# Four buffers for expert results, and the gather of the fifth expert ahead issued before each scatter

## The reference

```
h      = rmsnorm(x1, g_ffn)                                   # 512 x 1024
scores = sigmoid(h @ w_router)                                # 64 experts
top_idx = top_k(scores + router_bias, 8);  gates = normalised scores * 2.5
y  = sum over experts e of  gates[:, e] * (silu(h @ w_gate_e[e]) * (h @ w_up_e[e])) @ w_down_e[e]
y += (silu(h @ w_gate_s) * (h @ w_up_s)) @ w_down_s           # shared expert
out = x1 + y
```

## Time and profile before

| | us |
|---|---|
| median of 3 runs (1119.38 to 1122.89) | 1120.4 |
| the profiled execution | 1125.33 |
| its span, first to last instruction | 1123.3 |
| TensorE busy with matmuls | 1089.0 (97%) |
| VectorE busy | 881.5 (78%) |
| ScalarE busy | 738.1 (66%) |
| GpSimd busy | 326.3 (29%) |

### The profile page before, as it was taken

The page is one execution under the profiler, slowest core; times in us unless marked ns, Lnnn a source line. Parts: engine busy times, 40 slices in busy tenths (PEclk is TensorE's granted clock), DMA queues, the critical chain, the costliest instruction groups (busy, mean ns, idle before and its releaser), DMA issues.

```text
span 1123.3 us, 19070 instructions
## 1 busy us (share of the span) xinstructions
PE 1089.0 (97%) x5809; PEld 894.5 (80%) x5809; DVE 881.5 (78%) x1405; ACT 738.1 (66%) x1304; POOL 326.3 (29%) x293
## 2 busy tenths in 40 slices
PE   7999999999999999999999999999999999999995
PEld 6789978777777887478888788888888788888884
DVE  6544385578766835589999999999998999999993
ACT  5434465444446422268888888888888888888883
POOL 1221021000000001126336633333344545534543
PEclk9999999999999999999999999999999999999998
DMA  7243211421522185459999999999999999999962
GB/s 245 77 110 111 81 52 63 150 76 48 159 77 95 62 341 209 171 229 400 374 383 377 376 376 392 381 371 369 375 374 376 380 365 369 375 382 376 376 202 36
DMA packets 69704, 284.69 MB, mean 253 GB/s; under 512 B 16611, under 2 KB 19179, under 8 KB 44700
## 3 DMA queue, kind: packets, MB, share of 16 engines
q1 hardware_dynamic: 51228, 250.50, 57.3%
q0 software_dynamic: 18432, 33.61, 12.8%
HBM read 279.79 MB, written 37.81 MB: 283 GB/s over the span
## 4 chain that ended last, share of the span: by engine, by line
DMA 49%; PE 32%; DVE 7%; issue 5%; POOL 3%; ACT 2%; POOLq 1%; SPq 0%; ACTq 0%; DVEq 0%
DMA out<-arena,idxs 48%; PE bank L1647 21%; PE bank L1795 3%; POOL turn L592 2%; PE bank L1591 2%; PE bank L1809 2%; DVE w_lo L1082 1%; ACT arena L782 1%; DMA arena<-in_w_in 1%; DVE gu_parts L1433 1%; PE bank L1703 1%; PE bank L1716 1%; PE bank L1905 1%; ACT w_hi L681 1%; PE bank L1692 1%
## 5 line engine op out<-in xcount | busy, mean ns | idle before, releaser
L1821 PE MATMUL bank<-gu_parts,xT_parts 128*128 128x512 f32 x1280 | 339.0, 395 | 3.3 <-DVE xT_parts L1426 1.6
L1821 PEld LDWEIGHTS bank<-gu_parts,xT_parts 128*128 128x128 f32 x1280 | 235.3, 188 | 51.0 <-DVE xT_parts L1426 2.7
L1835 PE MATMUL bank<-w_lo 128*128 128x512 f32 x804 | 201.5, 399 | 1.0 <-DVE w_lo L1439 1.0
L592 POOL TENSOR_TENSOR turn<-minus_half 16x1 f32<-16x1 f32 x128 | 101.6, 794 | 345.8 <-DMA out<-arena,idxs 292.7
L1835 PEld LDWEIGHTS bank<-w_lo 128*128 128x128 f32 x804 | 146.3, 188 | 29.7 <-DVE w_lo L1439 1.1
L1647 PE MATMUL bank<-w_hi,hT_hi 128*128 128x512 f32 (+1 forms) x320 | 125.0, 391 | 2.3 <-DVE w_lo L1082 2.3
L1647 PE MATMUL bank<-w_hi,hT_lo 128*128 128x512 f32 (+1 forms) x320 | 122.5, 383 | 0.0
L1647 PE MATMUL bank<-w_lo,hT_hi 128*128 128x512 f32 (+1 forms) x320 | 122.1, 382 | 0.0
L602 POOL DMA_INDIRECT out<-arena,idxs x64 | 110.4, 1725 | 26.7 <-issue 23.8
L1433 DVE TENSOR_TENSOR gu_parts<-arena_x,gu_parts 128x1024 fp32r<-128x1024 f32 x96 | 117.0, 1218 | 1.3 <-ACT gu_parts L953 1.2
L1433 DVE TENSOR_TENSOR gu_parts<-arena,gu_parts 128x1024 fp32r<-128x1024 f32 x96 | 117.0, 1219 | 0.0
(11 more groups left out here) (226 smaller groups left out, 1958.4 us busy)
## 6 DMA issues: line engine op xcount, KB each, us to landing
arena<-in_w_gate_e SPq DMA_DIRECT2D x32, 1024.0 KB, 8.9
arena<-in_w_up_e SPq DMA_DIRECT2D x32, 1024.0 KB, 12.3
arena<-in_w_down_e SPq DMA_DIRECT2D x32, 1024.0 KB, 7.4
arena_x<-in_w_gate_e SPq DMA_DIRECT2D x32, 1024.0 KB, 9.0
arena_x<-in_w_up_e SPq DMA_DIRECT2D x32, 1024.0 KB, 12.2
arena_x<-in_w_down_e SPq DMA_DIRECT2D x32, 1024.0 KB, 7.1
arena<-in_w_in SPq DMA_DIRECT2D x14, 1024.0 KB, 5.4
arena<-in_w_gate SPq DMA_DIRECT2D x8, 1024.0 KB, 5.8
```

Source lines behind the costliest of these rows:

```text
L592: nc.gpsimd.tensor_tensor(turn[:], minus_half[0:16, 0:1], minus_half[0:16, 0:1], ALU.add).then_inc(turns, 1)
L1821: last = nc.tensor.matmul(out_, a[:, PER * c + j, :], b[c][:, :, j, :], start=(c == 0 and j == 0 and i == 0), stop=(c == CHUNKS - 1 and j ...
L1835: last = nc.tensor.matmul(psY[h][0:rows, :], midT[n][a][:, j, 0:rows], w[b][:, j, h * 512:(h + 1) * 512], start=(j == 0 and k == 0), stop= ...
```

## The change

Results get two more buffers: one at 20 KB of the arena, and a new tile `y_more` in the space that the tile `w_lo` has and the expert stage doesn't need. `pos` gets a tile of its own, since 23 KB is now under a result buffer. ScalarE's `y_i` takes the slot in place of the parity and waits for experts 0 to k-4 in place of 0 to k-2; the wait of `keep_idx` stays as it is. In GpSimd's `pair` the gather of expert k+5 stands before the scatter of expert k, with the numbers of their turns exchanged.

```diff
--- before.py
+++ after.py
@@ -177,6 +177,7 @@
         idxs = [sb(f"idxs{i}", [P, 1], u32) for i in range(4)]
         hn_ss, hn_ms, hn_r = sb("hn_ss", [P, NT]), sb("hn_ms", [P, NT]), sb("hn_r", [P, NT])
         rbias = sb("rbias", [P, E])
+        pos = sb("pos", [P, NT, E])[:]
 
         KB = 256
         with ExitStack() as view_ctx:
@@ -186,7 +187,9 @@
         arena = sb("arena", [P, 121 * KB])
 
 
-        w_lo = sb("w_lo", [P, RING, N], mybir.dt.float32r)
+        with ExitStack() as lo_ctx:
+            w_lo = lo_ctx.enter_context(nc.sbuf_tensor("w_lo", [P, RING, N], mybir.dt.float32r))
+        down_parts, y_more = sb("down_parts", [P, 20 * KB], mybir.dt.float32r), sb("y_more", [P, 4 * KB])
         with ExitStack() as split_ctx:
             hT_hi, hT_lo, w_hi = (split_ctx.enter_context(nc.sbuf_tensor(name, [P, blocks, N], mybir.dt.float32r))
                                   for name, blocks in (("hT_hi", ND), ("hT_lo", ND), ("w_hi", RING)))
@@ -250,11 +253,10 @@
 
         wgu = [at(k, 2 * ND * F).rearrange("p (g j c) -> p g j c", g=2, j=ND) for k in (40, 121, 153, 0)]
         wd = [at(k, NF * D).rearrange("p (j c) -> p j c", j=NF) for k in (56, 137, 169, 64)]
-        y = [at(24 + 4 * i, D) for i in range(2)]
+        y = [at(24, D), at(28, D), at(20, D), y_more[:]]
         xg = [at(72 + 4 * i, D) for i in range(4)]
         table = at(145, NT * E * 3).bitcast(bf16).rearrange("p (t e c) -> p t e c", t=NT, e=E)
 
-        down_parts = w_lo[:].rearrange("p b c -> p (b c)")
         wd_hi, wd_lo = (down_parts[:, i * NF * D:(i + 1) * NF * D].rearrange("p (j c) -> p j c", j=NF) for i in range(2))
         last_hi, last_lo = (gu_parts[:, k * KB:k * KB + NF * D].rearrange("p (j c) -> p j c", j=NF) for k in (8, 16))
         midT = [[down_parts[:, 2 * NF * D + (2 * i + k) * NF * P:2 * NF * D + (2 * i + k + 1) * NF * P].rearrange("p (j s) -> p j s", j=NF)
@@ -271,7 +273,6 @@
         sel, rep, M, gt, gres = (at(16 + i, NT * E).rearrange("p (t e) -> p t e", t=NT) for i in range(5))
         scores = at(24, NT * E).rearrange("p (t e) -> p t e", t=NT)
         Mb = at(22, NT * E // 2).bitcast(bf16).rearrange("p (t e) -> p t e", t=NT)
-        pos = at(23, NT * E).rearrange("p (t e) -> p t e", t=NT)
         wr = at(112, ND * E).rearrange("p (j e) -> p j e", j=ND)
 
         bank = [ctx.enter_context(nc.psum_tensor(f"bank{i}", [P, 512], f32)) for i in range(8)]
@@ -612,7 +613,7 @@
                 pool.wait_ge(y_ready, 2 * (SH + k + 1))
                 pool.wait_ge(idx_kept, k + 1)
                 after(pool, scattered, 16 * k)
-                scatter(u % 2, idxs[u], before, scattered)
+                scatter(u, idxs[u], before, scattered)
 
             for k in range(5):
                 gather_k(k, k % 4, k)
@@ -620,8 +621,8 @@
                 pool.wait_ge(b, 8 * SH)
 
             def pair(k, u):
-                scatter_k(k, u, 5 + 2 * k)
-                gather_k(k + 5, (u + 1) % 4, 6 + 2 * k)
+                gather_k(k + 5, (u + 1) % 4, 5 + 2 * k)
+                scatter_k(k, u, 6 + 2 * k)
 
             for k in range(4):
                 pair(k, k)
@@ -925,11 +926,11 @@
                 after(act, mid_ready, it - 1)
                 silu_of(n).then_inc(silu_ready, 1)
 
-            def y_i(it, n):
-                after(act, scattered, 16 * (it - SH - 1))
+            def y_i(it, slot):
+                after(act, scattered, 16 * (it - SH - 3))
                 for h in range(2):
                     act.wait_ge(y_psum, 2 * it + h + 1)
-                    copy_y(n, h).then_inc(y_ready, 1)
+                    copy_y(slot, h).then_inc(y_ready, 1)
 
             def midT_i(it, n, rows):
                 act.wait_ge(midT_psum, it + 1)
@@ -979,12 +980,12 @@
                     for h in range(2):
                         split_wd(slot, h, last_hi).then_inc(wd_hi_ready, 1)
                     midT_i(it, n, SLOTS)
-                    y_i(it - 1, 1 - n)
+                    y_i(it - 1, (slot + 3) % 4)
                     return
                 if more:
                     xT_hi_k(k + 1)
                     gu_hi_k(k + 1, (slot + 1) % 4, CHUNKS - 1)
-                y_i(it - 1, 1 - n)
+                y_i(it - 1, (slot + 3) % 4)
                 midT_i(it, n, SLOTS)
                 wd_i(it, slot)
 
@@ -1023,7 +1024,7 @@
                     step(4 * m + u, u % 2, u)
             for it in range(ITEMS - 4, ITEMS):
                 step(it, it % 2, it % 4, more=it + 1 < ITEMS)
-            y_i(ITEMS - 1, 1)
+            y_i(ITEMS - 1, 3)
 
             more = act.value_load(rounds_i[0:1, 0:1], min_val=0, max_val=ROUNDS - 1)
             with act.If(more > 0):
```

## The result

The changed kernel takes 1187.5 us (median of 6 runs, 1166.98 to 1192.61), the kernel before, on the same chip, 1120.9 (6 runs, 1116.65 to 1125.38): **slower, by a ratio of 1.0466 [1.0421, 1.0511]**. The prediction was 1109 us, range 1105 to 1121, with 0.65 for faster. The sign, the size and the range are wrong. The profiled execution took 1187.38, a span of 1185.4, which is 62.1 us over the span of before.

A forecast was written before the change was run, and what follows sets the result against it. It took TensorE's 9.53 us a step, plus scatter-chain delays through ScalarE, as the bound. Minus 13.1 and +1.0 for slips gave -12.1 on 1125.3, 1113.2; runs' median 4.9 lower, 1108.3, taken as 1109 us, range 1105 to 1121.

The forecast's parts named there:

- The reading of the bound: Expert stage: TensorE's 9.53 us a step bounds it, plus what the scatter chain adds through ScalarE; 13.1 us lost.
- The two limits: ScalarE's waits for scatters: the result copy's goes, `keep_idx` is next in line, so room gained is 3.65 us.
- After, it settles by itself: Scatter chain: late scatters are followed sooner, so offsets settle near 4.5 to 5, below the new limit of 7.2; minus 13.1 us.
- -13.1 us for free steps: Expert stage: the sixty steps run at TensorE's 9.53 us each once ScalarE no longer holds them, saving 13.1 us.
- The moved gather: GpSimd's gather in front of the scatter: hidden with over 3 us to spare; +0.6 us from scatter 1, taken up by the room.
- The end: Last scatters: the end follows the steps one for one; a chain 2 us late is made good there.
- The rule weighed: VectorE instructions with two SBUF inputs lock out GpSimd instructions reading SBUF; one GpSimd turn of 5.83 us agreed.
- Rival 1: Scatter chain keeps 9.81 us a link whatever its offset, so 3.65 us is won once: 1116.7 us; chance 0.15.
- Rival 2: DMA transfers are the bound, so faster steps only lengthen the landings: 1120.4 us, no change; chance 0.10.
- Rival 3: A scatter's turn, held by VectorE's two-input operations, slips a whole step and ScalarE is held: 1130 to nearer 1140; chance 0.17.

The follow-up runs named there:

- e3: The changed kernel with `keep_idx` moved behind the result copy of its step in ScalarE's order: 1125.6 us.
- e11: e3 with scatter k also waiting for VectorE's eighth gu_lo of expert k+3: within 1125 to 1130 us.
- e12: e3 with scatter k also waiting on `wd_ready` for VectorE's low parts of the down weights, a hold that caught little beyond scatter 0: 1127.6 us.
- e5: The changed kernel, loading only an eighth of the down weights from expert 4 on (its output is not the layer): 1112.4 us.
- e2: The kernel before with only GpSimd's new order, gather in front of scatter, and two buffers as before: 1127.2 us.
- e9: The changed kernel with only ScalarE's old limit put back, the result copy waiting for the scatter two before: 1125.9 us.
- e13: e3 with scatter k also waiting for both down_lo of expert k+3, which closes a loop of waits: landing 10.2 us, time not given.
- e14: e3 with scatter k also waiting for the first down_lo of expert k+3, which closes a loop of waits: landing 10.3 us, time not given.

## Why the prediction was wrong

- **The reading of the bound** held half. The path of the loss was right: a held ScalarE, VectorE behind it, a late step. But I took TensorE's 9.53 us a step as the bound and the chain as a disturbance of it. It is the other way round: at full load the link is 9.74 us or more on average in every kernel here, above 9.53, and in all of them ScalarE runs up against it. So the chain of scatters is the bound, and buffers between a slower consumer and a faster producer fill up however many there are.
- **The two limits** were right. The result copy's wait is gone, `keep_idx` is the next in line, TensorE's waits for gathers are gone.
- **"After, it settles by itself" is the step that failed.** The falling link (10.17 us early, 9.38 late) was real, but it was read at offsets up to some 6 us, and in a kernel whose steps the old limit was drawing out. I drew it on beyond, to a limit at 7.2, and took it over into a kernel without that limit. With the limit lifted, scatters 5 to 6 us behind the burst are followed after 9.7 to 9.8 us (e3, e11, e12), where before it was 9.0: the short links that were to settle the chain below 9.53 are not there. And where the next burst is 9.5 us behind the last, there was too little room between good and bad: scatters 1 to 4 started 5.0 to 6.2 us behind the transposes, three of them with an instruction of 2.2 to 2.4 us, the fourth landed in 11.3 us, the fifth started at 8.7, and from then on the median offset is 10.9, on the burst, with links of 10.96 over the stage. One long landing was enough to leave the good place, and nothing led back. 56 x (10.96 - 9.53) is 80 us that the sum had at nothing.
- **-13.1 us for free steps** was too large as well, by 4: e5, in which the scatters hold nobody, is 8.7 us faster than before. (The slow step of the earlier trace rows is the next one after the held copy, not the next but one.)
- **The moved gather**: hidden, as said. At the start it cost 1.4 us of scatter 1, where I had 0.6. What I had at nothing is that GpSimd's turns fall otherwise against VectorE: from 500 us on they are over 1.5 us long 7 times before, 10 times in e2 and 19 times in e9. Those are the two kernels with the new order and the old limit, and they lie 0.5 and 0.4% over before. That this is the cause was not tried.
- **The end** did not follow the steps alone: it is the chain's, 5.4 us shorter from scatter 57 on, because that scatter started 3 us behind the issue of the last loads and landed in 5.2 us, where before it took 10.4.
- **The rule weighed**, the lock of two-input operations, stood in for the wrong risk. From 500 us on, one turn of the changed kernel was held for more than 1.5 us.
- **Rival 1** (the chain keeps its link) had the right mechanism for a chain that is the bound and lacked the phase; its 1116.7 is wrong. **Rival 2** is wrong in its time and right that the load and the chain belong together: e5, at 292 GB/s, is the only kernel whose link (9.50) goes under 9.53 us. But the transfers fell to 334 GB/s here, so their rate was not the bound. **Rival 3** had the sign, 1130 to 1140, a slip of a scatter past a point and a ScalarE held behind it; but its trigger (a held turn) did not occur, and the price was 10.96 us a link and not 10.17. None of the three had a landing that depends on the loads, although the two link lengths of the early and late scatters asked for a cause.
- The question left out was what makes an early scatter slow. Sorting the same 57 by their distance to SyncE's issues, which the timeline of before shows, would have given 9.4 us at 3 to 4 and 8.1 at 5 to 6, and two questions: what comes at 9, and whether the 8.1 stays when the steps are no longer held.

The Trainium skill ("DMA: Bandwidth & Descriptors", Queues, rings and completion order) says that a DMA engine takes turns between the queues that have work, a packet at a time. By that a scatter should be slower whenever SyncE's queue has work; the rows agree in kind (4.7 us behind the last loads, a mean of 8.8 beside them), but at a DMA share of 1.02 the engines are busy throughout, so the rule alone gives no difference of phase. Where the 1.2 us come from inside the DMA engines stays open: I have their sum, not their order. The page of the Trainium skill "DMA: Bandwidth & Descriptors" (SWDGE vs HWDGE vs iDMA) also says that GpSimd writes the descriptors of its DMAs into SBUF, and that VectorE locks it out of SBUF while in a 2-port mode. The operations beside the 2.40 us have two inputs in SBUF, for which the page says nothing of the kind, so the 2.40 us against 1.59 show a delay of that sort outside its rule.

## What to carry to other kernels

More buffers help only where the consumer's rate is above the producer's; in these kernels a chain that is the bound drifted to whatever limit stood, and the buffers only chose where it came to rest. Before moving a limit, work out the place of rest, and look up what else starts there in the same period: here a wait 3.65 us later put each scatter beside a burst of loads. A rate that varies with an offset is not to be drawn past the range in which it was read, nor taken over into a kernel without the limit under which it was read; and where the kernel repeats every 9.5 us, the offset is one on a circle.

## What the runs showed of the hardware

- A scatter with addition from GpSimd (an index list of 128 entries, of which 64 on average are tokens of 4 KB) is under way, its 1.59 us of issue not counted, 6.1 to 7.8 us when it starts 4 to 6 us behind the issue of 2 MB of loads on SyncE's queue, and 8.5 us or a little more when it starts within 1 us of it (load at full pace), though before moves some 375 GB/s and the changed kernel 335. Once the loads are over a scatter lands in 4.6 us in all.
- Its issue takes 1.59 us on GpSimd, and about 2.40 where VectorE is already in an operation with two SBUF inputs when it starts (262 of 263 long ones); where such an operation starts 0.4 us later it stays at 1.59.
- In e13 and e14, whose TensorE was busy for 76 and 81 of the 100 us from 700 to 800, the granted clock of that stretch was 0.89 and 0.91 on average, where e3, busy for 99, reads 1.00.
- No kernel tried that does the whole work beats the one before. The nearest, e3, e9, e11, e12 and e2, lie 0.3 to 0.5% above it.
